# Attention scores of four mLSTM heads: fp32 products, or three rounded passes from split queries and keys

## The reference, cut to what matters

```python
s = jnp.einsum('bhjd,bhsd->bhjs', qc, kc) * w_intra
num = (jnp.einsum('bhjs,bhsd->bhjd', s, vc)
       + w_inter[..., None] * jnp.einsum('bhvk,bhjk->bhjv', C, qc))
...
C_new = decay[..., None, None] * C + jnp.einsum('bhs,bhsv,bhsk->bhvk', w_s, vc, kc)
```

## Time and profile before

| | us |
|---|---|
| median of 3 executions | 941.85 (941.04 to 942.53) |
| the profiled execution | 942.27, its span 940.7 |
| TensorE busy | 928.3 (99%) |
| VectorE busy | 772.2 (82%) |
| ScalarE busy | 464.4 (49%) |
| GpSimd busy | 106.7 (11%) |

### The profile page before, as it was taken

One profiled execution on the slowest core, in us unless ns is written; L12 is line 12 of the kernel. 1 busy time (PEld: TensorE's weight loads), 2 busy tenths in 40 slices (PEclk: granted clock), 3 DMA queues, 4 the chain that ended last, 5 costly groups with the idle time before them and its releaser, 6 DMA issues. The chain is left out here.

```text
span 940.7 us, 18449 instructions
## 1 busy us (share of the span) xinstructions
PE 928.3 (99%) x6833; PEld 907.8 (96%) x6833; DVE 772.2 (82%) x1231; ACT 464.4 (49%) x684; POOL 106.7 (11%) x110
## 2 busy tenths in 40 slices
PE   8999999999999999999999999999999999999996
PEld 8999999999999999999999999999999999999995
DVE  6899985988698869876455569999888999889997
ACT  6654452445336324634833345456545555455664
POOL 3011330042006001500231000000000000000001
PEclk9999999999999999999999999999999999999998
DMA  6245216211620352042342222233222223232122
GB/s 219 68 150 198 69 57 224 90 45 56 246 90 23 134 191 90 23 150 87 117 140 68 89 73 84 90 108 106 102 90 91 90 68 113 90 116 109 46 91 100
DMA packets 22460, 98.56 MB, mean 105 GB/s; under 512 B 2929, under 2 KB 5122, under 8 KB 17909
## 3 DMA queue, kind: packets, MB, share of 16 engines
q1 hardware_dynamic: 19576, 77.13, 24.9%
q0 software_dynamic: 1984, 19.72, 5.7%
q10 hardware_dynamic: 832, 0.88, 0.3%
HBM read 85.28 MB, written 12.44 MB: 104 GB/s over the span
## 5 line engine op out<-in xcount | busy, mean ns | idle before, releaser
L1301 PE MATMUL ps<-h_hi,w_hi 128*128 128x288 f32 x896 | 193.7, 298 | 0.0
L1301 PE MATMUL ps<-h_lo,w_hi 128*128 128x288 f32 x896 | 191.7, 295 | 0.0
L1301 PE MATMUL ps<-h_hi,w_lo 128*128 128x288 f32 x896 | 191.4, 295 | 0.0
L793 ACT ACTIVATE w_hi<-raw 128x1024 fp32r<-128x1024 f32 x76 | 80.4, 1058 | 177.4 <-PE ps L1301 174.2
L1301 PEld LDWEIGHTS ps<-h_hi,w_hi 128*128 128x128 f32 x896 | 143.5, 189 | 1.3 <-issue 0.6
L1301 PEld LDWEIGHTS ps<-h_hi,w_lo 128*128 128x128 f32 x896 | 144.3, 189 | 0.0
L1301 PEld LDWEIGHTS ps<-h_lo,w_hi 128*128 128x128 f32 x896 | 144.2, 188 | 0.0
L1692 DVE TENSOR_TENSOR w_lo<-raw,w_hi 128x1024 fp32r<-128x1024 f32 x76 | 94.2, 1240 | 48.9 <-ACT w_hi L793 48.8
L1917 DVE SCALAR_TENSOR_TENSOR conv<-a_p,vec,conv x120 | 97.6, 813 | 0.2
L1569 PE MATMUL ps<-cols_b,late 128*128 128x288 f32 x432 | 62.8, 295 | 0.1
L1569 PE MATMUL ps<-cols_a,main 128*128 128x288 f32 x432 | 62.9, 295 | 0.0
(11 more groups left out here) (362 smaller groups left out, 1857.3 us busy)
## 6 DMA issues: line engine op xcount, KB each, us to landing
raw<-w_head_in SPq DMA_DIRECT2D x40, 512.0 KB, 3.5
raw<-w_fp_in SPq DMA_DIRECT2D x18, 1024.0 KB, 4.9
cs<-st_c_in POOLq DMA_DIRECT2D x4, 2048.0 KB, 9.6
c_s_out<-cs POOLq DMA_DIRECT2D x4, 2048.0 KB, 7.7
raw<-w_fo_in SPq DMA_DIRECT2D x8, 1024.0 KB, 4.9
x<-xT_in SPq DMA_DIRECT2D x16, 288.0 KB, 4.1
raw<-w_cgcv_in SPq DMA_DIRECT2D x8, 512.0 KB, 3.6
raw<-w_ga_in SPq DMA_DIRECT2D x8, 512.0 KB, 3.5
```

Of the source, the lines that this page charges most:

```text
L793: act.activation(w_hi[:, s, :], raw[:, s, :], ACT.Copy).then_inc(hi_ready, 1)
L1301: last = pe.matmul(ps[:, 2 * s + b, 0:HALF], wt[:, w, k * P:k * P + P], src[:, k, b * HALF:b * HALF + HALF], start=(k == 0 and wt is w_hi ...
```

## The change

1. Queries and keys are split like weights. ScalarE rounds the queries into `q_hi` behind unit 1 (two copies of 576 columns) and the keys into `k_hi` behind the decay weights (two of 512, one of 2 x 64 for the samples). VectorE subtracts, in place over queries and keys in `qkv`: two subtractions of 576 columns, two of 512, one of 2 x 64. `q_hi` lies over `cp` and `num`, `k_hi` over the place of the values in `kvn`.
2. The scores are made of rounded products: keys high by queries high, keys high by queries low, keys low by queries high, so 30 rounded products a head in place of 10 in fp32, after a wait for all five low parts.
3. Since the keys in `qkv` are overwritten, their transposes are made between unit 4 and unit 5, in three uses, and those of the values stay behind the scores, in three uses. ScalarE copies them with six instructions in place of five.
4. On VectorE the order is now: small copy of the samples' queries, the queries' low parts, four small copies into `qm`, the weights' low part for unit 6, a wait for the keys' transposes, the keys' low parts, the four taps that followed the weights' low part before, then the low part for unit 7 as before.
5. The wait for the buffer `cp` is made ahead of `q_hi`.

```diff
@@ -89,9 +89,9 @@
 
-S_USE, T_USE, I_USE, K_USE, PV_USE, CP_USE, CS_USE, N_USE, HT_USE = 0, 5, 10, 11, 13, 18, 20, 28, 29
-USES = 32
-READER = ["dve"] * 5 + ["act"] * (5 + 1 + 2 + 5 + 2) + ["dve"] * (8 + 1 + 3)
+TK_USE, S_USE, TV_USE, I_USE, K_USE, PV_USE, CP_USE, CS_USE, N_USE, HT_USE = 0, 3, 8, 11, 12, 14, 19, 21, 29, 30
+USES = 33
+READER = ["act"] * 3 + ["dve"] * 5 + ["act"] * (3 + 1 + 2 + 5 + 2) + ["dve"] * (8 + 1 + 3)
 ACT_USES, DVE_USES = READER.count("act"), READER.count("dve")
...
@@ -307,8 +307,12 @@
         wvs = nc.alloc_sbuf_tensor_at("wvs", [P, SB, HD], F32R, offset=head_base + 4 * 2 * T)
+        qk_lo = nc.alloc_sbuf_tensor_at("qk_lo", [P, 2, 2, T], F32R, offset=head_base)
         kvn_base = place[0]
         kvn = sb("kvn", [5, 2 * HD + 2])
+        cp = sb("cp", [2, VE])
+        q_hi = nc.alloc_sbuf_tensor_at("q_hi", [P, 2, T], F32R, offset=(place[0] - 4 * (2 * T - NB * VE)) // 32 * 32)
+        assert NB * VE < 2 * T <= (NB + 2) * VE
         num = sb("num", [5, VE])
...
@@ -333,6 +336,7 @@
         inter_lo = sb("inter_lo", HD)
+        q_samples = sb("q_samples", [2, TS])
         assert place[0] <= x_base + 4 * KT * T
@@ -340,6 +344,15 @@
         assert W_OFF[NB] <= RING * 2 * HD and NB * (VE + 1) <= RING * 2 * HD
+
+        def k_hi(k):
+            return kvn_lo[:, 0:NB, HD + k * P:HD + k * P + P]
+
+        def k_hi_samples():
+            return kvn_lo[:, NB, HD:HD + 2 * P].rearrange("p (k t) -> p k t", k=2)[:, :, 0:TS]
+
+        def of_prompt(t):
+            return t[:, 0:TP].rearrange("p (s t) -> p s t", s=NB)
 
...
@@ -905,6 +920,11 @@
                     evac_bias(h, j, halves(qkv[:, 0, :, :], j))
+                act.wait_ge(dve_read, h * DVE_USES + START)
+                act.wait_ge(cp_free, h + START)
+                for k in range(2):
+                    act.wait_ge(slot_read[k], h * (PER_HEAD // 2) + (C_B + 1))
+                    act.activation(q_hi[:, k, :], qkv[:, 0, k, :], ACT.Copy).then_inc(qk_hi_ready, 1)
                 hi_of(2)
@@ -923,9 +943,28 @@
                 hi_of(3)
-                for j in range(4, 6):
-                    hi_of(j)
-                    evac_bias(h, j, halves(qkv[:, 2, :, :], j - 4))
+                for k in range(2):
+                    act.wait_ge(slot_read[k], h * (PER_HEAD // 2) + (C_B + 2))
+                    act.activation(k_hi(k), of_prompt(qkv[:, 1, k, :]), ACT.Copy).then_inc(qk_hi_ready, 1)
+                act.activation(k_hi_samples(), qkv[:, 1, :, TP:T], ACT.Copy).then_inc(qk_hi_ready, 1)
+
+                def turned_rows(first_use, g, c):
+
+                    use(first_use + g)
+                    if g < NB // 2:
+                        act.activation(kvn[:, 2 * g:2 * g + 2, c:c + HD],
+                                       bank(first_use + g)[:, 0:2 * HD].rearrange("p (s c) -> p s c", s=2), ACT.Copy)\
+                            .then_inc(act_read, 1)
+                    else:
+                        act.activation(kvn[0:TS, NB, c:c + HD], bank(first_use + g)[0:TS, 0:HD], ACT.Copy)\
+                            .then_inc(act_read, 1)
+
+                hi_of(4)
+                evac_bias(h, 4, halves(qkv[:, 2, :, :], 0))
+                for g in range(3):
+                    turned_rows(TK_USE, g, 0)
+                hi_of(5)
+                evac_bias(h, 5, halves(qkv[:, 2, :, :], 1))
                 def old_hi(b):
@@ -936,10 +975,8 @@
                     old_hi(b)
-                for i in range(5):
-                    use(T_USE + i)
-                    n = P if i < NB else TS
-                    act.activation(kvn[0:n, i, 0:2 * HD], bank(T_USE + i)[0:n, :], ACT.Copy).then_inc(act_read, 1)
+                for g in range(3):
+                    turned_rows(TV_USE, g, HD)
 
...
@@ -965,7 +1002,6 @@
                     act.activation(num[0:n, i, :], bank(PV_USE + i)[0:n, 0:VE], ACT.Copy).then_inc(act_read, 1)
-                act.wait_ge(cp_free, h + START)
                 for k in range(2):
@@ -1367,7 +1403,7 @@
 
-                    samples = (S_USE + 4, T_USE + 4, PV_USE + 4, HT_USE + 2)
+                    samples = (S_USE + 4, TV_USE + 2, PV_USE + 4, HT_USE + 2)
                     if k + 1 in samples and k >= 3:
@@ -1385,28 +1421,41 @@
                 head_unit(0, beside=lambda k: pe.wait_ge(hlo_ready, k + 1))
-                for j in range(1, 6):
+                def turn_rows(first_use, of):
+
+                    for g in range(3):
+                        use(first_use + g)
+                        for t in range(2 * g, min(2 * g + 2, NB + 1)):
+                            n = P if t < NB else TS
+                            for c in range(2):
+                                o = t % 2 * HD + c * P
+                                last = pe.transpose(bank(first_use + g)[0:n, o:o + P],
+                                                    qkv[:, of, c, t * P:t * P + n], ident[:, :])
+                        last.then_inc(attn_ready, 1)
+
+                for j in range(1, 5):
                     head_unit(j)
-
                 for s in range(2):
                     pe.wait_ge(slot_read[s], h * (PER_HEAD // 2) + (C_B + 2))
+                turn_rows(TK_USE, 1)
+                head_unit(5)
+
+                pe.wait_ge(qk_lo_ready, h * 5 + 5)
                 for s in range(5):
...
                     for k in range(2):
-                        last = pe.matmul(bank(S_USE + s)[0:rows_, 0:n], qkv[:, 1, k, t0:t0 + rows_],
-                                         qkv[:, 0, k, t0:t0 + n], start=(k == 0), stop=(k == 1))
+                        of_hi = kvn_lo[:, s, HD + k * P:HD + k * P + rows_]
+                        of_lo = qk_lo[:, 1, k, t0:t0 + rows_]
+                        for keys, queries in ((of_hi, q_hi), (of_hi, qk_lo[:, 0]), (of_lo, q_hi)):
+                            last = pe.matmul(bank(S_USE + s)[0:rows_, 0:n], keys, queries[:, k, t0:t0 + n],
+                                             start=(k == 0 and keys is of_hi and queries is q_hi),
+                                             stop=(k == 1 and keys is of_lo))
                     last.then_inc(attn_ready, 1)
...
                     pe.wait_ge(slot_read[s], h * (PER_HEAD // 2) + (C_B + 3))
-                for s in range(5):
-                    use(T_USE + s)
-                    n = P if s < NB else TS
-                    for c in range(4):
-                        last = pe.transpose(bank(T_USE + s)[0:n, c * P:c * P + P],
-                                            qkv[:, 1 + c // 2, c % 2, s * P:s * P + n], ident[:, :])
-                    last.then_inc(attn_ready, 1)
+                turn_rows(TV_USE, 2)
 
@@ -1426,7 +1475,7 @@
                 for k in range(2):
-                    last = pe.matmul(bank(I_USE)[0:TS, HD:HD + SB], qkv[:, 0, k, TP:T],
+                    last = pe.matmul(bank(I_USE)[0:TS, HD:HD + SB], q_samples[:, k, :],
                                      nst[:, bass.ds(h, 1), k, :].rearrange("p o b -> p (o b)"),
@@ -1446,7 +1495,7 @@
                     if t == 0:
-                        read(T_USE + 4)
+                        read(TV_USE + 2)
                         pe.wait_ge(pvlo_ready, h * 2 + 2)
@@ -1941,14 +1990,31 @@
 
+                def by_sample(t):
+                    return t.rearrange("p (b j) -> p b j", b=SB)
+
                 for k in range(2):
                     evacuated(k, 1)
-                    steps.on(dve.tensor_copy(alone(0, k), qkv[:, 0, k, TP:T].rearrange("p (b j) -> p b j", b=SB)))
+                steps.on(dve.tensor_copy(q_samples[:, :, :], qkv[:, 0, :, TP:T]))
                 steps.settle()
+                dve.wait_ge(qk_hi_ready, h * 5 + 2)
                 for k in range(2):
-                    dve.tensor_tensor(alone(1, k), qkv[:, 0, k, TP:T].rearrange("p (b j) -> p b j", b=SB),
-                                      alone(0, k).bitcast(F32), ALU.subtract).then_inc(qm_ready, 1)
-                lo_of(4)
+                    dve.tensor_tensor(qk_lo[:, 0, k, :], qkv[:, 0, k, :], q_hi[:, k, :].bitcast(F32), ALU.subtract)\
+                        .then_inc(qk_lo_ready, 1)
+                for k in range(2):
+                    steps.on(dve.tensor_copy(alone(0, k), by_sample(q_hi[:, k, TP:T].bitcast(F32))))
+                dve.wait_ge(qk_lo_ready, h * 5 + 2)
+                for k in range(2):
+                    dve.tensor_copy(alone(1, k), by_sample(qk_lo[:, 0, k, TP:T].bitcast(F32))).then_inc(qm_ready, 1)
+                split_lo(h * PER_HEAD + (U_B + 6), 0)
+                use(TK_USE + 2)
+                dve.wait_ge(qk_hi_ready, h * 5 + 5)
+                for k in range(2):
+                    dve.tensor_tensor(of_prompt(qk_lo[:, 1, k, :]), of_prompt(qkv[:, 1, k, :]), k_hi(k).bitcast(F32),
+                                      ALU.subtract).then_inc(qk_lo_ready, 1)
+                dve.tensor_tensor(qk_lo[:, 1, :, TP:T], qkv[:, 1, :, TP:T], k_hi_samples().bitcast(F32), ALU.subtract)\
+                    .then_inc(qk_lo_ready, 1)
```

(14 more changed lines are left out.)

## The result

The changed kernel takes 946.53 us, the median of 12 executions (942.39 to 950.62), against 941.52 for the kernel before in 12 others (940.36 to 942.53): a ratio of 1.0048, with a 95% interval of 1.0036 to 1.0061. It is 0.48% slower. The forecast of 942.6 is missed and so is its range, which ended at 946.0.

The account below looks back on a forecast made before the run. TensorE was taken to bound the kernel. Four heads: 4 x (-0.77 + 0.34 + 0.11) + 2.05 = +0.8 us, so a median of 942.6 us; the forecast's own range was 941.4 to 943.9, the whole range 940.2 to 946.0.

Parts of the forecast that it names:

- What bounds the kernel: In the heads' loop a microsecond of TensorE work is a microsecond of time, other engines' work free until TensorE waits.
- Part 1: Scores in three rounded passes: per head the wide blocks -0.77 us, the narrow ones +0.34 us.
- Rivals 2 and 3: Narrow score products cost only columns, 1.5 us less (chance 0.07); or rounded under 256 columns run at fp32 rate, +4.1 (0.08).
- Part 2: Keys' transposes made a unit sooner, so in two turns: +0.11 us a head.
- Part 3: VectorE's new work ahead of the scores makes the fourth score block wait: +2.05 us in four heads.
- Rival 1: VectorE keeps up, no wait ahead of the fourth score block: -1.3 us, 940.6 us; chance 0.15.
- rival 4: GpSimd starts before unit 7's low part: 943.9 us for the first head alone (chance 0.11), 947.6 for all four (0.06).

Follow-up runs that it names:

- e9: Changed kernel with three convolution taps, two from ahead of unit 7's low part and one from behind it, moved behind unit 10's: 937.78 us, ratio 0.9962.
- e2: Changed kernel with two of VectorE's four convolution taps ahead of unit 7's low part moved behind unit 10's low part: 940.37 us, ratio 0.9988.
- e5_keys_sooner_fp32: Kernel before with only the keys' transposes made a unit sooner, scores in fp32 and no split: 942.18 us, ratio 1.0005.
- short execution: Changed kernel, nothing edited, the profiled execution from the group of four at 942.39 to 942.91 us: 942.91 us.
- long execution: Changed kernel run again, nothing edited, the profiled execution of that run: 947.1 us; the run's median is 946.97 us.
- e4_before_late_taps: Kernel before, fp32 scores, with three more convolution taps ahead of unit 7's low part and three fewer later in the head: 963.54 us, ratio 1.0227.
- e6_gpsimd_waits: Changed kernel with one wait added, GpSimd's first product only after VectorE's low part for unit 7: 943.43 us, ratio 1.0018.

## Why the prediction was wrong

**What bounds the kernel: right.** Outside the new waits TensorE's sum was the time, head by head: without them the heads are 87.8 to 88.3 us apart (`e9`, `e2`) for the 88.5 of before.

**Part 1, the price of the products: right.** The sum said -0.77 + 0.34 = -0.43 us a head (3.88 to 3.10 is -0.78, a slip of 0.01); the block without a wait shows 4.35 - 4.78 = -0.43. The spacings were forecast as 0.226, 0.172 and 0.118 for 512, 384 and 256 columns and are 0.234, 0.173 and 0.118; narrow products were put at 0.11 and 0.06 and are 0.11 and 0.058. Rivals 2 and 3 are false by that. The wait is what hid this: in the changed kernel itself the third head's fourth block comes 0.55 us after its forerunner where 0.12 would do.

**Part 2, the transposes: too high.** Forecast +0.11 us a head. TensorE in the third head of the changed kernel:

```profile
275.97 1.25 PE L1432 MATMUL ps<-ident,qkv 128*128 128x128 f32 x10
276.98 0.51 PE L1337 MATMUL ps<-h_hi,w_hi 128*128 128x288 f32 x2
...
288.08 1.31 PE L1432 MATMUL ps<-ident,qkv 128*128 128x128 f32 x10
289.15 0.48 PE L1470 MATMUL ps<-cs_hi,qm 128*128 128x256 f32 x2
```

They take 1.01 and 1.07 us, and the pair of unit products behind the first group is 0.08 longer than its neighbours: 2.16 for the 2.27 of before, -0.11 at this place. Over a whole head `e5_keys_sooner_fp32` shows 0.0 (88.51 us for 88.50), so some 0.1 is lost again among the other products. The term was 0.1 to 0.2 us a head too high, and no part of the miss.

**Part 3, VectorE's sum and the wait: right where nothing holds it.** VectorE in the third head of the changed kernel:

```profile
277.12 1.43 DVE L2002 TENSOR_TENSOR qk_lo<-qkv,q_hi 128x576 fp32r<-128x576 f32 x2
...
280.02 1.29 DVE L2013 TENSOR_TENSOR qk_lo<-qkv,kvn_lo 128x512 fp32r<-128x512 f32 x2
...
285.10 1.22 DVE L1741 TENSOR_TENSOR w_lo<-raw,w_hi 128x1024 fp32r<-128x1024 f32 x1
```

The pairs of 576 and 512 columns were put at 1.41 and 1.29 with their overlap. The wait, forecast as 1.06, 0.45, 0.27 and 0.27 us, is 1.25, 0.45, 0.42 and 0.44 in the short execution: 2.56 for 2.05, in the place that was named. Rival 1 is false. In the long execution the first head's wait is 4.2 in place of 1.25; that is the step that failed, told below.

**Two waits that I had at nothing.** I wrote that the later taps slip "and then VectorE waits for that unit anyway", and named a wait at the samples' split only as a sign of error. It came: K products wait for VectorE's `kv_lo` in heads 2 and 4 (0.7 us listed), and old-state products for GpSimd's `cs_lo` in heads 1 and 3 (0.4). About 0.3 us a head: the cover existed on average over the head and not at these two points.

With these corrections the short execution can be told nearly whole, with the -0.11 for the transposes. From one head's scores to the next it is 1.3 us longer over three heads (0.95 + 0.16 + 0.19): three times -0.43 - 0.11, 2.1 of waits ahead of the fourth block, 0.7 of the two waits not foreseen, which is +1.2. The first head's scores start 0.8 later, where the ten transposes alone add 1.1 (from the head's first product to them it is 39.5 for 38.4 us, so the heads' stage itself began 0.3 sooner); from the last head's scores to the end it is 1.6 shorter (569.1 for 570.7 us), where the moved transposes, the cheaper scores and the two waits give 0.8. So 0.3 and 0.8 us of gain outside the heads, in code that nobody edited, are unaccounted for. The forecast of +0.8 was near for this group of executions, whose four lie 0.9 to 1.4 us over the median of before, but in part by luck: the waits were put 0.5 and 1.1 us too low, and against that stand the transposes and the gain outside the heads.

**The step that failed is rival 4's place in the sum: its chance and its price.** GpSimd's hold of the low part for unit 7 was put at nothing in the sum, and got a chance of 0.11 for the first head at 1.25 us. I had the mechanism, the instruction, the head (the first, by a margin of 0.25 us) and the rows. Both start times came from one execution, and that one has TensorE at its slower rate. At this rate the margin is there, 0.10 us (107.79 and 107.89). At the faster rate GpSimd starts 0.6 us sooner and VectorE doesn't, so the order is turned round: GpSimd at 107.30, the low part due at 108.0. A margin of 0.25 us read from one execution didn't bear odds of one in nine. By their times eight executions of twelve are held.

The price was more than threefold too low. I took one product of GpSimd, 1.25 us, straight into the wait. Measured: first, two VectorE instructions are held one after the other, since GpSimd is free to start its next product between them, 2.1 us in place of 1.25. Second, what runs on after the wait is at half clock, 2.4 us that the sum had no term for. Kernel `e4_before_late_taps` shows the same terms over four heads: 3.0 us of lateness, 7.0 more of waits, 6.1 of clock. The range ended at 946.0 because it was meant to reach just over the 943.9 of one such head; with the right price that head gives 943.0 + 4.4 = 947.4 for the profiled execution, inside the group that was measured.

**What stays open.** Why TensorE makes the first head's products 0.133 us apart in one execution and 0.130 in another, at the same granted clock; this decides when GpSimd starts. Why the clock fell behind gaps of 1.97 and 1.95 us between starts in heads 2 and 3 of `e4_before_late_taps` but not behind the 1.98 of head 4, nor behind the 2.2 of `e6_gpsimd_waits`. And what makes the longest executions (949.2 and 950.62 us of the changed kernel), of which none was profiled.

## What to carry to other kernels

Where the sum shows an engine arriving within half a microsecond of another one that can hold it, price both orders, each with its full chain: every instruction that will be held in turn, the wait that comes of it, and TensorE's clock behind that wait. Such a race shows in the executions as two groups and not as a broad spread, so profile one of each before reading a median. And when a change puts work ahead of an instruction that TensorE waits for, move something else out of its way in the same edit: here three taps behind unit 10 turned 0.5% slower into 0.4% faster. Take the margin from more than one profile of the kernel before: here the one that was read had TensorE at the rate that hid the danger.

## What the runs showed of the hardware

- A VectorE instruction that GpSimd holds shows the hold as its own duration and not as idle time: 0.28 becomes 1.29, 0.75 becomes 1.75, 1.22 becomes 2.30, about 1.0 us each with GpSimd products of 128x512 in fp32. No list of waits names it. GpSimd, busy for a ninth of the span, cost 16.9 us of median in `e4_before_late_taps`, the clock behind the waits included.
- 0.1 us of order decided: starting 0.10 us ahead of GpSimd the low part took 1.22 us (107.79 and 107.89), starting 0.11 behind it 2.30 (202.25 and 202.14 in `e4_before_late_taps`). One tap (0.94 us) of work moved 5.2 us of median.
- TensorE made the same stretch of some 240 products of 288 columns in 32.0 or in 31.2 us, at a granted clock of 1.00 both times.
- In a stretch of 4.0 us without work TensorE's granted clock fell to 0.50, and it stayed there for 5.1 us after work came back. At that clock products of 128 columns are spaced 0.21 us (0.11 at full clock), those of 64 columns 0.11 (0.058), so narrow rounded products scale with the clock too.
- Three rounded passes for fp32 save 9% of such a score block (4.35 for 4.78 us), not 25%: a product of 128 columns costs 0.11 us, be it a rounded one or one of the two records of an fp32 one, so there it is three against two.
